# Causal masks of three query blocks moved from VectorE into TensorE's score matmuls, diagonal tiles first in a head, shorter statistics chains and a tail in halves

## The reference

```python
s = jnp.einsum('bhqd,bhkd->bhqk', q_blk, kt) * scale
s = jnp.where(k_idx[None, :] <= q_idx[:, None], s, -jnp.inf)      # causal mask
o = jnp.einsum('bhqk,bhkd->bhqd', jax.nn.softmax(s, axis=-1), vt)
...
o = (inner + cross)                                               # retention, then a norm per head
mu = jnp.mean(o, axis=-1, keepdims=True)
var = jnp.mean(jnp.square(o - mu), axis=-1, keepdims=True)
o = ((o - mu) * lax.rsqrt(var + EPS)) * gn_gain
...
x = x + g1 * rmsnorm(mix, post_norm_mix)                          # after the output projection
h = rmsnorm(x, pre_norm_ffn) * (1.0 + sc2) + sh2
x = x + g2 * rmsnorm((silu(h @ w_gate) * (h @ w_up)) @ w_down, post_norm_ffn)
```

## Time and profile before

| | |
|---|---|
| device time, median of 3 runs | 2041.57 us (2040.0 to 2043.76) |
| the profiled execution | 2044.0 us, its span 2042.1 us (core 7) |
| spans of the eight cores | 2026.6 to 2042.1 us |
| TensorE busy | 1926.2 us (94%), 10080 matmuls |
| VectorE, ScalarE, GpSimd busy | 885.8 (43%), 1035.5 (51%), 657.9 us (32%) |
| chain that ended last | TensorE 84%, of it 83% at L612 |

### The profile page before, as it was taken

One profiled execution on the slowest core, in us unless ns is written; L12 is line 12 of the kernel. 1 busy time (PEld: TensorE's weight loads), 2 busy tenths in 40 slices (PEclk: granted clock), 3 DMA queues, 4 the chain that ended last, 5 costly groups with the idle time before them and its releaser, 6 DMA issues.

```text
span 2042.1 us, 34016 instructions; the slowest of 8 cores (2026.6 to 2042.1 us)
## 1 busy us (share of the span) xinstructions
PE 1926.2 (94%) x10080; PEld 894.7 (44%) x10080; DVE 885.8 (43%) x1789; ACT 1035.5 (51%) x2076; POOL 657.9 (32%) x967
## 2 busy tenths in 40 slices
PE   1799999899999999999998899999999999999998
PEld 1455555444334444443444444444444444444443
DVE  3567777885233445577667423121221213131121
ACT  4655756569999999897786112121211212121111
POOL 2555666532222434355334432020302011020202
PEclk9999999999999999999999999999999999999999
DMA  9766765333101323334435855050312213040101
GB/s 293 230 156 157 167 161 125 107 87 109 44 22 60 94 57 112 83 102 138 144 88 146 205 123 136 11 145 1 109 37 74 72 42 104 11 144 11 52 11 42
DMA packets 111480, 204.83 MB, mean 100 GB/s; under 512 B 58920, under 2 KB 61896, under 8 KB 107080
## 3 DMA queue, kind: packets, MB, share of 16 engines
q1 hardware_dynamic: 107560, 176.97, 28.6%
q0 software_dynamic: 3744, 25.69, 7.2%
HBM read 165.57 MB, written 48.07 MB: 105 GB/s over the span
## 4 chain that ended last, share of the span: by engine, by line
PE 84%; issue 4%; DVE 3%; DMA 3%; ACT 3%; POOL 2%; SPq 0%; POOLq 0%; DVEq 0%; ACTq 0%
PE bank L612 83%; DMA waf<-w_ada 2%; PE bank L619 1%; ACT PT L588 1%; DMA Wd<-wd 1%; ACT yn L588 0%; SPq L582 0%; DVE hT L596 0%; DMA ckTb<-ck_scr 0%; ACT xn L588 0%; DVE PT L591 0%; DMA hT<-xn 0%; DVE bs L1069 0%; POOL rqk L591 0%; DVE mixt L599 0%
## 5 line engine op out<-in xcount | busy, mean ns | idle before, releaser
L588 ACT ACTIVATE PT<-bank 128x512 bf16<-128x512 f32 (+1 forms) x1088 | 555.8, 588 | 47.7 <-PE bank L612 41.7
L612 PE MATMUL bank<-PT,V 128*128 128x512 bf16 (+3 forms) x1152 | 385.7, 361 | 12.3 <-DVE PT L591 7.1
L612 PE MATMUL bank<-Q,KT 96*128 96x512 bf16 (+3 forms) x1152 | 391.8, 362 | 1.7 <-ACT PT L588 1.0
L588 ACT ACTIVATE sgt<-bank 128x512 bf16<-128x512 f32 x176 | 104.9, 597 | 471.1 <-PE bank L612 459.9
L612 PE MATMUL bank<-h2T,Wg 128*128 128x512 bf16 x1408 | 334.9, 380 | 3.1 <-DVE h1T L591 1.0
L612 PE MATMUL bank<-h2T,Wu 128*128 128x512 bf16 x1408 | 333.1, 379 | 1.0 <-DVE mixt L599 0.9
L612 PE MATMUL bank<-Wd,h1T 128*128 128x512 bf16 x1408 | 305.8, 379 | 1.0 <-DMA Wd<-wd 0.8
L591 DVE TENSOR_TENSOR h1T<-bank,sgt 128x512 bf16<-128x512 f32 x176 | 121.6, 691 | 393.9 <-PE bank L612 378.8
L612 PE MATMUL bank<-W,hT 128*128 128x512 bf16 (+2 forms) x1280 | 258.5, 356 | 16.5 <-DVE sg L599 4.8
L612 PEld LDWEIGHTS bank<-Wd,h1T 128*128 128x128 bf16 x1408 | 137.7, 98 | 167.6 <-issue 2.2
L612 PEld LDWEIGHTS bank<-h2T,Wg 128*128 128x128 bf16 x1408 | 137.2, 98 | 168.2 <-issue 7.0
(11 more groups left out here) (170 smaller groups left out, 2118.9 us busy)
## 6 DMA issues: line engine op xcount, KB each, us to landing
xt<-x SPq DMA_DIRECT2D x64, 512.0 KB, 5.0
x_scr<-xt SPq DMA_DIRECT2D x32, 512.0 KB, 2.9
xa<-x_scr SPq DMA_DIRECT2D x32, 512.0 KB, 4.7
xb<-x_scr SPq DMA_DIRECT2D x32, 512.0 KB, 4.0
out<-xb SPq DMA_DIRECT2D x32, 512.0 KB, 2.9
waf<-w_ada SPq DMA_DIRECT2D x4, 2048.0 KB, 31.6
wadab<-w_ada POOLq DMA_DIRECT2D x8, 1024.0 KB, 10.1
yg_scr<-yn SPq DMA_DIRECT2D x32, 256.0 KB, 3.1
```

What stands on the lines that cost most here:

```text
L588: return OP("act", lambda g: g.activation(out=out, in_=in_, func=func, **kw), r, w)
L612: x = g.matmul(out, lhsT=l, rhs=rh, start=st, stop=sp, **kw)
```

## The change

Four edits.

Masks: in blocks 2, 1 and 0 a diagonal tile's score matmul leaves its first 128 columns open and a matmul of `identb` with `lowb` (0 where a key is allowed, -1e9 where not) is added to them; VectorE's multiplication goes. In blocks 7 to 3 GpSimd still multiplies.

Order: in blocks 7 to 1 a head's items are now recorded as diagonal, full, diagonal, full, diagonal, full, and then the other full ones; the PVs as full, diagonal, and so on.

Statistics: in retention the add ahead of the pow goes to VectorE; in the output projection it goes to VectorE and ahead of the multiplication; in the feed-forward part two GpSimd operations become one.

Tail: in the last 128 tokens VectorE adds the second half, and each half has its own transfer.

```diff
+    lowb = S.buf("lowb", 128, BF16, pin=True)
+    ts("dve", lowb.v, trif.v, -1.0, ALU.add, 1e9, ALU.mult, [trif], [lowb])
...
-            tt("pool", gs.v[:, 0:4], bav[:, 1], sm("epw"), ALU.add, [ba, smallc], [(gs, 0)])
+            tt("dve", gs.v[:, 0:4], bav[:, 1], sm("epw"), ALU.add, [ba, smallc], [(gs, 0)])
...
-                stt(bag.v[:, 2:3], bag.v[:, 0:1], bag.v[:, 0:1], bag.v[:, 1:2], ALU.mult, ALU.add, [(bag, 0)], [(bag, 1)])
-                tt("pool", bag.v[:, 3:4], bag.v[:, 2:3], e2.v[:, j:j + 1], ALU.add, [(bag, 1), e2], [(bag, 2)])
+                tt("dve", bag.v[:, 2:3], bag.v[:, 1:2], e2.v[:, j:j + 1], ALU.add, [(bag, 0), e2], [(bag, 1)])
+                stt(bag.v[:, 3:4], bag.v[:, 0:1], bag.v[:, 0:1], bag.v[:, 2:3], ALU.mult, ALU.add, [(bag, 0), (bag, 1)], [(bag, 2)])
...
+            ks = [(h, kb, ((0, kb, 0),)) for kb in range(4 * s)]
+            ds = [(h, 4 * s, ((0, 4 * s, 0),)), (h, 4 * s + 1, ((0, 4 * s + 1, 128),)),
+                  (h, 4 * s + 2, ((0, 4 * s + 2, 256), (256, 4 * s + 3, 384)))]
+            if s:
+                for d, k in zip(ds, ks):
+                    items += [d, k]
+                    later += [k, d]
+                items += ks[3:]
+                later += ks[3:]
...
+                if kb >= 4 * s and s < 3:
+                    lst = [(PS[bk][:, o + 128:o + 512 - c0], kt, q[:, 128:], True, True, {})] if c0 < 384 else []
+                    lst += [(PS[bk][:, o:o + 128], kt, q[:, 0:128], True, False, {}), (PS[bk][:, o:o + 128], identb.v, lowb.v, False, True, {})]
...
-            if k0 >= 4 * s:
+            if k0 >= 4 * s >= 12:
-                tt("dve" if s < 3 else "pool", v, v, bcast(trib.v, [[0, n], [1, 128]]), ALU.mult, [pt, trib], [pt])
+                tt("pool", v, v, bcast(trib.v, [[0, n], [1, 128]]), ALU.mult, [pt, trib], [pt])
...
-                y = ahead.pop(0)
+                y = ahead.pop(later[i - LOOK])
...
-            tt("pool", st.v[:, 2:3], st.v[:, 0:1], st.v[:, 1:2], ALU.add, [(st, 0), (st, 1)], [(st, 2)])
-            ts("pool", st.v[:, 2:3], st.v[:, 2:3], EPS, ALU.add, 1.0, ALU.mult, [(st, 2)], [(st, 2)])
+            ts("pool", st.v[:, 2:3], st.v[:, 0:1], st.v[:, 1:2], ALU.add, EPS, ALU.add, [(st, 0), (st, 1)], [(st, 2)])
...
-                tt("pool", xt.v[:, hs], xt.v[:, hs], t_.v[:, hs], ALU.add, [(xt, hf), (t_, hf)], [(xt, hf)])
-            dma("sp", dr["out"][tb * 128:(tb + 1) * 128, :], xt.v, r=[xt], w=[(outD, tb)])
+                end = si == NSB - 1 and j == 3
+                tt("dve" if end and hf else "pool", xt.v[:, hs], xt.v[:, hs], t_.v[:, hs], ALU.add, [(xt, hf), (t_, hf)], [(xt, hf)])
+                if end:
+                    dma("sp", dr["out"][tb * 128:(tb + 1) * 128, hs], xt.v[:, hs], r=[(xt, hf)], w=[(outD, (tb, hf))])
+            if not end:
+                dma("sp", dr["out"][tb * 128:(tb + 1) * 128, :], xt.v, r=[xt], w=[(outD, tb)])
```

More of the change, by code:

```diff
@@ L1463, in record @@
         q0 = s * 512
-        items = []
+        items, later, first_last = [], [], {}
         for h in range(8):
[L1466 to L1469, removed]
+            ks = [(h, kb, ((0, kb, 0),)) for kb in range(4 * s)]
+            ds = [(h, 4 * s, ((0, 4 * s, 0),)), (h, 4 * s + 1, ((0, 4 * s + 1, 128),)),
+                  (h, 4 * s + 2, ((0, 4 * s + 2, 256), (256, 4 * s + 3, 384)))]
+            n = len(items)
+            if s:
[4 more added lines that the diff above has]
+                later += ks[3:]
+            else:
+                items += ds
+                later += ds
+            ends = later[n], later[-1]
+            first_last[h] = ends
         nL, nF = len(items), len(fill)
@@ L1479, in emit_S @@
             for o, kb, c0 in parts:
-                last["s"] = mm([(PS[bk][:, o:o + 512 - c0], KT[t][h // 4].v[0:96, h % 4 * 512 + (kb % 4) * 128:h % 4 * 512 + (kb % 4 + 1) * 128],
-                     Qcur.v[0:96, h * 512 + c0:(h + 1) * 512], True, True, {})],
-                   [(KT[t][h // 4], h), (KT[t][h // 4], "pe"), (Qcur, (h, 0)), (Qcur, (h, 1))], [PSB[bk]])
+                kt, q = KT[t][h // 4].v[0:96, h % 4 * 512 + (kb % 4) * 128:h % 4 * 512 + (kb % 4 + 1) * 128], Qcur.v[0:96, h * 512 + c0:(h + 1) * 512]
+                lst = [(PS[bk][:, o:o + 512 - c0], kt, q, True, True, {})]
+                if kb >= 4 * s and s < 3:
+                    lst = [(PS[bk][:, o + 128:o + 512 - c0], kt, q[:, 128:], True, True, {})] if c0 < 384 else []
+                    lst += [(PS[bk][:, o:o + 128], kt, q[:, 0:128], True, False, {}), (PS[bk][:, o:o + 128], identb.v, lowb.v, False, True, {})]
+                last["s"] = mm(lst,
+                   [(KT[t][h // 4], h), (KT[t][h // 4], "pe"), (Qcur, (h, 0)), (Qcur, (h, 1)), identb, lowb], [PSB[bk]])
                 cols = o + 512 - c0
@@ L1498, in emit_PV @@
                 vo = (kb % 4) * 768 + (h // 2) * 192 + (h % 2) * 64
-                mm([(PS[ab][:, c0:512], Vt[t].v[:, vo:vo + 128], pt.v[:, o:o + 512 - c0], kb == 0, kb == 4 * s + 3, {})], [Vt[t], pt], [PSB[ab]])
+                mm([(PS[ab][:, c0:512], Vt[t].v[:, vo:vo + 128], pt.v[:, o:o + 512 - c0], x[0] is first_last[h][0] and o == 0,
+                     x[0] is first_last[h][1] and (o, kb) == parts[-1][:2], {})], [Vt[t], pt], [PSB[ab]])
         pair_t = {}
@@ L1522, in record @@
         heads_acc = {}
-        ahead = []
+        ahead = {}
         for i in range(nL + LOOK):
@@ L1526, in record @@
                 x = emit_S(items[i])
-                ahead.append(x)
+                ahead[items[i]] = x
             if i >= LOOK:
-                y = ahead.pop(0)
+                y = ahead.pop(later[i - LOOK])
                 h = y[0][0]
@@ L1534, in record @@
                 emit_PV(y, heads_acc[h])
-                if y[0][1] == 4 * s + 2:
+                if y[0] is first_last[h][1]:
                     head_end(h, heads_acc[h])
```

## The result

Beside the kernel before on the same chip, the changed kernel's time is 1.0038 times as long, interval [1.0023, 1.0053], which is some 8 us; the first comparison, with two executions (2048.8 and 2065.15 us), had given 1.0072 [1.0046, 1.0098]. The profiled execution took 2048.8 us, its span is 2047.2 us (core 7). By the ratio the changed kernel stands at some 2049 us; the forecast was 2037.0 us, with a range from 2031.0 to 2044.5. Some executions of an eight-core program run slower on one die whatever the kernel; they are left out throughout.

A forecast was written before the change was run, and what follows sets the result against it. TensorE's work plus its gaps was taken as the bound. Masks +5.4, waits -6.0, work behind masks -2.5, order 0, statistics -0.4, tail -1.1 made -4.6 us: 2037.0 us against the 2041.57 median, range 2031.0 to 2044.5.

The forecast's parts named there:

- shortened distance: Rival, blocks 7 to 1: 168 off-diagonal PVs follow their scores too soon; at 60 ns each, 2047.1 us; chance 0.15.
- the 56 ns: Blocks 2 to 0: TensorE time per added 128-column mask matmul, taken from transposes; 96 of them cost 5.4 us.
- the fourth rival: Blocks 2 to 0: short matmuls cost the full weight load, 12.3 us instead of 5.4, giving 2043.9 us; chance 0.07.
- The waits they remove: Blocks 2 to 0: of TensorE's 7.1 us waiting for VectorE masks, 6.0 us gained; ends 3.0 and 7.1.
- the 2.5 us behind the masks: Blocks 2 to 0: gain from VectorE work queued behind masks (mixt, h1T), of 4.8 us in reach; ends 0 and 4.8.
- the even trade: Rival, blocks 2 to 0: exps and banks nearly as late, only 3.0 us of waits goes; +1.3 us, 2042.9 us; chance 0.20.
- Order: Diagonal tiles first in blocks 7 to 1: costed at 0; lower end -1.3 us, upper end the third rival's price.
- third rival: Same as shortened distance: PVs in blocks 7 to 1 wait for exps, short by 0.32 us each; chance 0.15.
- Statistics: Shorter chains in retention and output projection: 0.4 us gained, from part of the mixt waits; ends 0 and 1.5 us.
- Tail: After the last matmul: dropped GpSimd operation and split adds gain 1.1 us; ends 0.9 and 1.25 us.
- the forecast's nearest row: Tail: VectorE's half of the add priced like its 128x512 product h1T, 0.69 us.
- the later of the two ends in the forecast: Tail: VectorE's add ends at 2037.82 if it must wait for GpSimd, against 2037.05 if undisturbed.

The follow-up runs named there:

- a_swap: Changed kernel at its own addresses, but down-weight tiles Wd2 and Wd5 change places, taking Wd2 off G1b; 0.9996 of the kernel before.
- a_place: Changed kernel with the buffer addresses of the kernel before, lowb made from trib ahead of block 2; 0.9996 of the kernel before.
- p_mt: Kernel before, at its own addresses, with only the TensorE masks (diagonal tiles last) and the split tail; 0.9978 of the kernel before.
- p_mask: Kernel before, at its own addresses, with only the TensorE masks of blocks 2 to 0, diagonal tiles last; 0.9988 of the kernel before.
- a_last: Changed kernel with diagonal tiles last everywhere and an address plan of its own; 0.9967 of the kernel before.
- p_ord3: Changed kernel at the kernel before's addresses, diagonal tiles first in blocks 2 and 1 alone; 0.9973 of the kernel before.
- a_out: Changed kernel with four gate and up steps moved behind the last output projection, own plan, weights and G1b unmoved; 1.0009 of the kernel before.

## Why the prediction was wrong
**The step that failed** is the sum itself: it priced every edit in the old plan, and the plan is made anew. The text knew it ("or if the plan, which is made anew, moves work elsewhere") and gave it neither a place, nor a price, nor a chance: the stretch from the last Wo matmul to the first output stood in the sum at nothing, and it grew by 8.8 us, 7.5 of them a longer wait for Wd. The traces of before would have given them: Wd was the last late wait before the feed-forward part (0.84 us), behind three loads issued at the end of the output projection. The prediction called the stretch from 1206 us on free of gaps and did not look at what stood just before it. Of the four rivals none was this one, and the slower one (shortened distance) is not what made it slower.

**The edits' own worth** is the time with the placement undone: a_swap -1.5 us, a_place +0.8 (both some 1.0 us more with the 11 matmuls), against -4.6 in the sum. So the sum would have missed without the plan as well. Masks and tail came nearly as priced: 5.4 - 6.0 - 2.5 - 1.1 = -4.2 us, measured -3.0 in the cuts of p_mt and some -4.5 by its ratio. What they gave is lost again with order and statistics, which stood at -0.4 and took 3.8 us (p_mt to a_place); that is the second part of the sum that failed.

**Masks.** 96 masks came in, 168 matmuls more (10248 against 10080). The pace in the changed kernel, starts of one run:
```profile
1052.81 0.22 PE L612 MATMUL bank<-lowb,identb 128*128 128x128 bf16 x1
1052.87 0.22 PE L612 MATMUL bank<-Q,KT 96*128 96x128 bf16 x1
1052.93 0.22 PE L612 MATMUL bank<-lowb,identb 128*128 128x128 bf16 x1
1052.98 0.38 PE L612 MATMUL bank<-PT,V 128*128 128x512 bf16 x1
```
50 to 60 ns each, and over the whole trace the median from a mask to the next start is 58 ns, so the 56 ns held and the fourth rival falls. The Trainium skill, TensorE: Matmul & The Clock Gate, section Back-to-back issue gap, gives 81 ns; this trace disagrees with it for masks as for transposes.

**The waits they remove** were oversized. Block 3's end to the last Wo matmul in p_mask, its window and waits of TensorE, and then two waits that the kernel before has there beside those of the earlier trace rows:
```profile
942.80:1186.80 244.00, 227.14 (x1366) 113.30 (x1365) 127.84 (x221) 144.35 (x252) 105.95 (x127) 0.99 0.53 143
PE bank L612 <- ACT PT L588: 3.4, 10, 0.8
PE bank L612 <- ACT sgt L588: 3.3, 5, 1.2
PE bank L612 <- POOL bag L591: 3.1, 1, 3.1
PE bank L619 <- issue: 2.8, 2, 2.4
```
```profile
PE bank L612 <- POOL bag L591: 3.1, 1, 3.1
PE bank L612 <- ACT sgt L588: 1.1, 2, 0.9
```
Of the 7.1 us for masks, 1.7 came back as waits for exps (1.7 to 3.4), 2.2 as waits for `sgt` (1.1 to 3.3); the gap without a releaser stayed (2.3 to 2.8 us). TensorE's gaps in this stretch went from 22.8 (245.6 - 222.84) to 16.9 us (244.0 - 227.14): -5.9 where 6.0 + 2.5 were forecast. The term furthest off is the 2.5 us behind the masks: `mixt`, `h1T` and the gap without a releaser went from 4.8 to 4.1 us (0.7 + 0.6 + 2.8). The stretch is 2.3 us shorter by the medians, where these terms make -3.1 and the even trade +2.4. Two readings of the prediction need a word. Its 0.23 and 0.89 us for a mask mix shapes; with GpSimd idle a mask took 0.20 to 0.23 us for 128 columns and 0.28 to 0.29 for 256, so the stretching is real. And the clock, passed over at 0.99, is 0.97 in this stretch on cores 3, 4 and 5 of the same execution: an estimated loss of 7 us at most (0.03 x 248), as TensorE had gaps then too.

**Order.** Priced at 0; what it costs as a whole stays open, as said above. It was not without effect in blocks 7 to 3 of the changed kernel: gaps of 10.9 us (515.50 - 504.58) instead of 4.9 (511.70 - 506.78). The third rival's waits for exps are 1.8 us of this, and GpSimd's masks still 1.0 us; the largest, 3.2 us, is for a transfer:
```profile
PE bank L612 <- DMA yg<-yg_scr: 3.2, 2, 2.0
PE bank L612 <- ACT PT L588: 1.8, 4, 0.8
PE bank L612 <- POOL PT L591: 1.0, 2, 0.8
```
a_last, with the diagonal last and its own plan, has gaps as large (518.80 - 508.70 = 10.1 us on its slowest core), so in a new plan they cannot be put down to the order alone. At the old addresses they can. Blocks 7 to 3 of a_place and then p_ord3, core 1 of both:
```profile
424.20:937.70 513.50, 503.09 (x2481) 215.94 (x2482) 253.22 (x360) 476.05 (x938) 183.81 (x247) 1.00 0.27 79
420.30:934.80 514.50, 509.23 (x2513) 216.92 (x2512) 258.84 (x369) 481.04 (x944) 184.25 (x249) 1.00 0.27 79
```
The gaps are 10.4 us with the diagonal first and 5.3 with it last, and waits for exps 2.4 us and none. So the third rival's mechanism is there, at 2 to 3 us and not at 10; from first PV to end the two kernels are level all the same.

**Statistics** 0.4 us forecast; alone, nothing that can be told. **Tail** 1.1 us forecast; 0.6 measured in the changed kernel, 0.7 in p_mt, 0.9 in a_place. Timeline of the changed kernel's tail, as in the earlier trace rows:
```profile
2040.55 1.41 DVE L599 SCALAR_TENSOR_TENSOR t<-bank,st,G2b 128x512 f32<-128x512 f32 x2 [7.78 <-POOL st L591]
2041.50 1.26 POOL L591 TENSOR_TENSOR xb<-xb,t 128x512 f32<-128x512 f32 x1 [1.06 <-DVE t L599]
2042.13 1.19 DVE L591 TENSOR_TENSOR xb<-xb,t 128x512 f32<-128x512 f32 x1 [0.17 <-DVE t L599]
2042.92 1.11 SPq L582 DMA_DIRECT2D out<-xb  x2
```
VectorE's half took 1.19 us, where the forecast's nearest row had 0.69, and ended 0.56 us after GpSimd's, the later of the two ends in the forecast. The second issue starts 0.78 us behind the first (1.11 - 0.33), where the forecast's early end had 0.33. The wait for GpSimd is what the rule cited from the Trainium skill (SBUF — State Buffer, section SBUF: two separate sides) says, and the trace agrees.

## What to carry to other kernels
In a kernel whose plan is made by a program, an edit buys a new plan, and here two plans of the same code differ by 7 to 16 us, while no edit moved more than some 5. So run an edit on the old addresses before judging it, and price the plan beforehand by the loads that are already nearly late: for each prefetch, what lies in its place, who reads that last, and how many microseconds of cover are left. Where a large tile must go over something that is read late, let it be the smallest one that is wanted last.

## What was not expected of the hardware
One wait of 8.4 us halved the granted clock for the 3.6 us behind it and cost an estimated 2.8 us in all, while three waits of 0.5 to 1.6 us in the same place, 3.2 us together, left it at 1.00. And a load issued 10.5 us earlier landed only about 9 us earlier (a_out): its down-weight loads took from 9.3 to 20.9 us to land, the longest the one issued last, behind three others in the same queue. In both kernels the DMA engines were busy all the time from its issue to its landing (a share of 0.96 to 1.03 in the windows).
